# Block table of a state-space layer: stationary and moving operands exchanged, transpose and replication rearranged

## What is computed

```
a_bar = exp(lam * dt)                      # 64 groups x 64 states, complex
b_bar = ((a_bar - 1) / lam) * b
x_t   = a_bar * x_{t-1} + b_bar u_t
y_t   = real(c x_t) + d * u_t
```

## Time and profile before

| | before |
|---|---|
| median of 3 runs | 1712.96 us (1708.61 to 1714.38) |
| the profiled execution | 1714.38 us, span of its trace 1712.3 us |
| PE busy | 1648.0 us, 96% |
| PEld busy | 1381.5 us, 81% |
| DVE busy | 1108.1 us, 65% |
| ACT busy | 945.7 us, 55% |
| POOL busy | 161.4 us, 9% |
| PE on the chain that ended last | 81% of the span |

### The profile page before, as it was taken

How to read it: one execution, slowest core, us unless ns; L and a number is a source line. 1 busy time by engine, 2 the same in 40 slices (tenths; PEclk the granted TensorE clock), 3 DMA queues, 4 the chain that set the end, 5 groups by cost and what they waited for, 6 DMA issues and landing times.

```text
span 1712.3 us, 22507 instructions
## 1 busy us (share of the span) xinstructions
PE 1648.0 (96%) x8994; PEld 1381.5 (81%) x8994; DVE 1108.1 (65%) x1566; ACT 945.7 (55%) x1576; POOL 161.4 (9%) x192
## 2 busy tenths in 40 slices
PE   9999999998999999999989999999999989999997
PEld 7788799786887787878768888788889889788886
DVE  5555667779677554868665556655557686655555
ACT  6455566654567685451465556755555554555545
POOL 0000000208001122710010000100000000000000
PEclk9999999999999999999989999999999999999999
DMA  6755443553455454441445555465554423455552
GB/s 239 265 183 189 169 153 144 179 197 148 174 195 184 176 187 147 180 172 51 160 154 197 178 194 186 158 222 186 194 188 157 148 100 128 176 196 190 187 188 98
DMA packets 50200, 295.93 MB, mean 173 GB/s; under 512 B 5976, under 2 KB 12592, under 8 KB 16432
## 3 DMA queue, kind: packets, MB, share of 16 engines
q1 hardware_dynamic: 49648, 293.86, 47.9%
q0 software_dynamic: 160, 0.52, 0.1%
q10 hardware_dynamic: 288, 0.11, 0.0%
HBM read 293.39 MB, written 1.09 MB: 172 GB/s over the span
## 4 chain that ended last, share of the span: by engine, by line
PE 81%; DVE 9%; ACT 6%; issue 2%; DMA 1%; SPq 1%; POOL 1%; DVEq 0%; POOLq 0%; ACTq 0%
PE PS L2064 77%; DVE wlo L1282 2%; PE PS L2287 2%; DVE wlo L1288 1%; ACT whi L717 1%; PE PS L2209 1%; DMA raw<-in_w 1%; ACT SC L924 1%; ACT whi L721 1%; PE PS L2067 1%; DVE SC L1746 1%; ACT wk L756 0%; PE PS L2460 0%; DVE X L1374 0%; ACT SC L1152 0%
## 5 line engine op out<-in xcount | busy, mean ns | idle before, releaser
L1288 DVE SCALAR_TENSOR_TENSOR wlo<-raw,ct,whi 128x512 fp32r<-128x512 f32 (+1 forms) x552 | 429.5, 827 | 288.0 <-ACT whi L721 287.7
L2064 PE MATMUL PS<-whi,xhi 128*128 128x512 f32 (+2 forms) x1328 | 514.0, 396 | 12.9 <-DVE wlo L1288 4.6
L721 ACT ACTIVATE whi<-raw,ct 128x512 fp32r<-128x512 f32 (+1 forms) x552 | 378.0, 734 | 246.1 <-PE PS L2064 203.5
L2064 PE MATMUL PS<-wlo,xhi 128*128 128x512 f32 (+2 forms) x1328 | 503.9, 389 | 0.0
L1282 DVE TENSOR_TENSOR wlo<-raw,whi 128x1024 fp32r<-128x1024 f32 x240 | 300.0, 1257 | 226.9 <-ACT whi L717 226.2
L2064 PE MATMUL PS<-whi,xlo 128*128 128x512 f32 (+2 forms) x1328 | 413.2, 389 | 0.0
L717 ACT ACTIVATE whi<-raw 128x1024 fp32r<-128x1024 f32 x240 | 252.1, 1057 | 270.7 <-PE PS L2064 201.6
L2064 PEld LDWEIGHTS PS<-whi,xhi 128*128 128x128 f32 x1328 | 251.1, 190 | 68.7 <-issue 8.5
L2064 PEld LDWEIGHTS PS<-whi,xlo 128*128 128x128 f32 x1328 | 251.5, 190 | 52.0
L2064 PEld LDWEIGHTS PS<-wlo,xhi 128*128 128x128 f32 x1328 | 252.2, 190 | 48.0
L2064 PE MATMUL PS<-whi,hhi 128*128 128x512 f32 x544 | 174.4, 395 | 5.2 <-DVE hlo L1453 5.2
(11 more groups left out here) (275 smaller groups left out, 1516.2 us busy)
## 6 DMA issues: line engine op xcount, KB each, us to landing
raw<-in_w SPq DMA_DIRECT2D x263, 1024.0 KB, 4.8
gr<-in_rows SPq DMA_DIRECT2D x14, 512.0 KB, 3.7
SC<-scratch SPq DMA_DIRECT2D x1, 2048.0 KB, 9.9
SC<-scratch SPq DMA_DIRECT2D x2, 1024.0 KB, 9.9
X<-in_x SPq DMA_DIRECT2D x2, 512.0 KB, 5.4
raw<-in_w SPq DMA_DIRECT2D x2, 512.0 KB, 7.1
xn<-in_sc SPq DMA_DIRECT2D x2, 512.0 KB, 3.9
out<-xn SPq DMA_DIRECT2D x4, 256.0 KB, 2.0
```

The source lines that it names most:

```text
L721: e = a.activation(hi[:, f], src[:, f], ACT.Copy, scale=ct[:, c:c + 1])
L1288: e = v.scalar_tensor_tensor(lo[:, f], src[:, f], ct[:, c:c + 1], hi[:, f].bitcast(f32), MUL, SUB)
L2064: return pe.matmul(o, l, r, start=start, stop=stop)
```

## The change

The matmuls of the table exchange their operands: `cst` (128 columns) is now stationary, and `c0` (32 columns) moves. The result for a pair is then 128 partitions (step s, channel) by 32 columns, already in the orientation of `kb`, so the block transpose of VectorE goes. VectorE instead builds `dd` for 16 pairs at a time on 32 partitions and adds it to the tau = 0 part on the way from PSUM into `kb`. ScalarE copies tau = 1 to 3 from PSUM to their places (6 copies of 32x512 for each half), and then the tau = 0 block to the three other places on the diagonal (3 copies). The steps of the tasks move, and the array of d is laid out in another way on the host (the same size as before).

```diff
@@ scalar, tables()
             def tables():
                 for _ in range(6):
                     yield
-                for _ in range(6):
-                    yield
                 for i in range(2):
+                    P = slice(16 * i, 16 * i + 16)
+                    kp = PS[:, 7, :].rearrange("p (i n) -> p i n", i=16)
+                    for _ in range(10):
+                        yield
+                    q.wait_ge(s_kp, i + 1)
+                    q.wait_ge(s_zk, 1)
+                    for tau in range(1, T):
+                        for s in range(T - tau):
+                            r = 32 * (T - 1 - tau)
+                            e = a.activation(kb[32 * s:32 * s + 32, P, s + tau, :], kp[r:r + 32], ACT.Copy)
+                        if tau == T - 1:
+                            e.then_inc(s_k5, 1)
+                        yield
                     q.wait_ge(s_k0, i + 1)
-                    q.wait_ge(s_zk, 1)
-                    for n in range(4):
-                        for s in range(T):
-                            src = ktau[i][32 * n:32 * n + 32, :, s:T, :][:, :, ::-1, :]
-                            e = a.activation(kb[32 * s:32 * s + 32, 16 * i + n:16 * i + 16:4, s:T, :], src, ACT.Copy)
-                            if s % 2:
-                                if n == 3 and s == 3:
-                                    e.then_inc(s_kb, 1)
-                                yield
+                    for s in range(T - 1):
+                        e = a.activation(kb[32 * s:32 * s + 32, P, s, :], kb[96:128, P, T - 1, :], ACT.Copy)
+                    e.then_inc(s_kb, 1)
+                    yield
@@ vector, tables()   (after step 6, which negates c0)
-                q.wait_ge(l_id, 16)
-                after_own()
-                link(v.tensor_reduce(one32, idt.rearrange("p (e c) -> p c e", e=4), AX.X, ADD))
-                tt(dd, one32[:, None, :].to_broadcast([128, 8, 32]), dsk[:, 0:8, None].to_broadcast([128, 8, 32]), MUL)
-                for _ in range(5):
-                    yield
                 for i in range(2):
+                    P = slice(16 * i, 16 * i + 16)
+                    kp = PS[:, 7, :].rearrange("p (i n) -> p i n", i=16)
+                    q.wait_ge(l_id, 16)
+                    if i:
+                        q.wait_ge(s_k0, i)
+                    tt(dd[96:128], idt[96:128, None, 96:128].to_broadcast([32, 16, 32]), dsk[96:128, P, None].to_broadcast([32, 16, 32]), MUL)
+                    for _ in range(9):
+                        yield
                     q.wait_ge(s_kp, i + 1)
-                    v.transpose(ktau[i].rearrange("p q s n -> p (q s n)"), PS[:, 7, :]).then_inc(s_kt, 1)
-                    q.wait_ge(s_kt, i + 1)
-                    tt(ktau[i][:, :, T - 1, :], ktau[i][:, :, T - 1, :], dd[:, 4 * i:4 * i + 4, :], ADD, s_k0)
-                    for _ in range(6):
+                    q.wait_ge(s_zk, 1)
+                    tt(kb[96:128, P, T - 1, :], kp[96:128], dd[96:128], ADD, s_k0)
+                    yield
+                    for _ in range(4):
                         yield
@@ tensor, tables()
             def tables():
-                for _ in range(7):
+                for _ in range(6):
                     yield
                 q.wait_ge(s_sp, 4)
                 q.wait_ge(s_c0, 1)
                 for i in range(2):
                     if i:
-                        q.wait_ge(s_kt, 1)
-                    for n in range(4):
+                        q.wait_ge(s_k0, 1)
+                        q.wait_ge(s_k5, 1)
+                    for n in range(16):
                         for k in range(2):
-                            for m in range(4):
-                                j = 16 * i + 4 * n + m
-                                r = cst[:, k, j, :, :].rearrange("p s n -> p (s n)")
-                                e = mm(PS[32 * m:32 * m + 32, 7, 128 * n:128 * n + 128], c0[k][:, j, :], r, k == 0, k == 1)
-                        if n == 3:
+                            l = cst[:, k, 16 * i + n, :, :].rearrange("p s n -> p (s n)")
+                            e = mm(PS[:, 7, 32 * n:32 * n + 32], l, c0[k][:, 16 * i + n, :], k == 0, k == 1)
+                        if n == 15:
                             e.then_inc(s_kp, 1)
                         if n % 2:
                             yield
-                    for _ in range(4 - i):
-                        yield
-                for _ in range(10):
-                    yield
-                q.wait_ge(s_kt, 2)
-                q.wait_ge(s_kb, 2)
+                    for _ in range(6):
+                        yield
+                q.wait_ge(s_k0, 2)
+                q.wait_ge(s_k5, 2)
                 for i in range(0, 32, 2):
```

More of the change, by code:

```diff
@@ L277, in program @@
             ("sc", "add", "max", "exp", "rc", "at", "pt", "aT", "av", "sq", "r", "on", "xt", "oh", "ol"))
-        s_turn, s_rho, s_e1, s_rot, s_dec, s_sc, s_c0, s_k0, s_kt, s_wT, s_xr, m_gg, m_av2, m_sf = (
-            sem(n) for n in ("s_turn", "s_rho", "s_e1", "s_rot", "s_dec", "s_sc", "s_c0", "s_k0", "s_kt", "s_wT", "s_xr", "m_gg", "m_av2", "m_sf"))
+        s_turn, s_rho, s_e1, s_rot, s_dec, s_sc, s_c0, s_k0, s_k5, s_wT, s_xr, m_gg, m_av2, m_sf = (
+            sem(n) for n in ("s_turn", "s_rho", "s_e1", "s_rot", "s_dec", "s_sc", "s_c0", "s_k0", "s_k5", "s_wT", "s_xr", "m_gg", "m_av2", "m_sf"))
         s_vc, s_gc, s_sin, s_zc, s_zk, s_sp, s_kp, s_kb, s_wt, s_wl, s_cst = (
@@ L374, in program @@
         g_t1 = p16(SC[:, small_at + 64:small_at + 64 + 512])
-        cut = Cut(4096)
-        ktau = [cut(512).rearrange("p (q s n) -> p q s n", q=4, s=T) for _ in range(2)]
-        dd, one32 = p32(cut(256)), cut(32)
+        dd = p32(SC[:, small_at + 64:small_at + 64 + 512])
         uS = xn.rearrange("p h (i n) -> p h i n", i=32)
@@ L1018, in tables @@
                     yield
-                for _ in range(6):
-                    yield
-                for i in range(2):
-                    q.wait_ge(s_k0, i + 1)
-                    q.wait_ge(s_zk, 1)
-                    for n in range(4):
-                        for s in range(T):
-                            src = ktau[i][32 * n:32 * n + 32, :, s:T, :][:, :, ::-1, :]
-                            e = a.activation(kb[32 * s:32 * s + 32, 16 * i + n:16 * i + 16:4, s:T, :], src, ACT.Copy)
-                            if s % 2:
-                                if n == 3 and s == 3:
-                                    e.then_inc(s_kb, 1)
-                                yield
+                for i in range(2):
+                    P = slice(16 * i, 16 * i + 16)
[11 more added lines that the diff above has]
+                        yield
+                    q.wait_ge(s_k0, i + 1)
+                    for s in range(T - 1):
+                        e = a.activation(kb[32 * s:32 * s + 32, P, s, :], kb[96:128, P, T - 1, :], ACT.Copy)
+                    e.then_inc(s_kb, 1)
+                    yield
                 for i in range(0, 32, 2):
@@ L1696, in tables @@
                 yield
-                q.wait_ge(l_id, 16)
-                after_own()
-                link(v.tensor_reduce(one32, idt.rearrange("p (e c) -> p c e", e=4), AX.X, ADD))
-                tt(dd, one32[:, None, :].to_broadcast([128, 8, 32]), dsk[:, 0:8, None].to_broadcast([128, 8, 32]), MUL)
-                for _ in range(5):
-                    yield
-                for i in range(2):
-                    q.wait_ge(s_kp, i + 1)
-                    v.transpose(ktau[i].rearrange("p q s n -> p (q s n)"), PS[:, 7, :]).then_inc(s_kt, 1)
-                    q.wait_ge(s_kt, i + 1)
-                    tt(ktau[i][:, :, T - 1, :], ktau[i][:, :, T - 1, :], dd[:, 4 * i:4 * i + 4, :], ADD, s_k0)
-                    for _ in range(6):
+                for i in range(2):
+                    P = slice(16 * i, 16 * i + 16)
[6 more added lines that the diff above has]
+                        yield
+                    q.wait_ge(s_kp, i + 1)
+                    q.wait_ge(s_zk, 1)
+                    tt(kb[96:128, P, T - 1, :], kp[96:128], dd[96:128], ADD, s_k0)
+                    yield
+                    for _ in range(4):
                         yield
@@ L2923, in layout @@
     dsk = np.zeros((128, 32), np.float32)
-    dsk[:, 0:8] = i["ssm_d"][0].reshape(8, 4, 32).transpose(1, 2, 0).reshape(128, 8)
+    dsk[:, :] = np.tile(i["ssm_d"][0].reshape(32, 32).T, (4, 1))
     par = np.stack([st(i["ssm_lam_re"][0]), st(i["ssm_lam_im"][0]), ldt, dsk])
```

## The result

The changed kernel takes 1723.49 us in the median of 4 runs (1721.64 to 1726.32), the kernel before 1713.07 us (1708.61 to 1714.38). The ratio is 1.0059, with a 95% interval of 1.0038 to 1.0081: slower by some 10 us (6.5 to 14). Forecast were 1723.8 us. Five more executions of the changed kernel are on record, from 1717.20 to 1724.95 us; the median of all nine is 1721.64 us.

A forecast was written before the change was run, and what follows sets the result against it. TensorE, busy in all of 26.00 us from 605 to 631, was taken as the bound. At 0.111 us a row, 14.2 - 3.4 = +10.8 us on the median 1712.96 gave 1723.8 us, range 1719 to 1728.

The forecast's parts named there:

- The price of a row: TensorE's table products: a row costs 0.111 us, set by the load of 128 stationary columns; bounds 0.027 and 0.125.
- the rival in which moving columns set the price: Table products: load hidden, a row costs 0.027 to 0.06 us, total 1713 to 1717 us; chance 0.08.
- All of it on the path: Work inserted into TensorE's program behind about 586 us moves the end one for one, unless it removes a wait.
- The sum for the back part: From the first down unit on: 14 steps of eight rows cost 12.4 us, in place of 3.6 us for three old bursts.
- The front: Before the first down unit: TensorE waits for negated `c0`, then runs 16 rows, and begins that unit 1.95 us late.
- rival at 0.18: TensorE's clock falls after the new gap of about 1.8 us, losing 1.7 us: 1725.5 us; chance 0.18.
- the slack of 5.4 us: ScalarE's spare time in splitting weights, so its bunched copies cost nothing; rival of late ScalarE: 2.5 to 5 us more, 0.06.
- VectorE and GpSimd: VectorE's new work, about 2.7 us for 2.8, and GpSimd's later end, with about 30 us of cover left, cost nothing.

The follow-up runs named there:

- copies twice: The kernel after with each of ScalarE's twelve table copies out of PSUM made twice, the second into free memory; ratio 1.0126 to the kernel before.
- single steps: The kernel before with transposes into wl only in steps no other transposes follow at once, the second step behind a down unit left empty; ratio 0.9992.
- the last one: The kernel before with the second step behind a down unit left empty and each table half in one burst of 64 rows; ratio 0.9979.

## Why the prediction was right

The mechanism held: products that lie on TensorE's path in full, at the price of a load of 128 columns, and a wait for `c0` in front. That the median of four executions lies only 0.3 us from the forecast is luck, for the interval of the difference is 6.5 to 14 us, and the parts of the sum were off by some 0.4 us in the back part and up to 0.7 us in the front.

**The price of a row** was the main term, and it held: 0.111 us predicted from products with 64 moving columns, 0.111 measured with 32. The reason given was the load of 128 columns. Doubling the moving side changed the back part by 0.02 us, halving the stationary side brought the row to 0.059; that refutes the rival in which moving columns set the price. That it is the load, and nothing else that grows with the stationary columns, rests on the loads' own records: 192 ns for 128 columns and 137 for 64, so 0.055 us for 64 columns. The 60 cycles that the Trainium skill names as the floor of a matmul (TensorEngine Tiling (Array Packing), Instruction Overhead), an estimate of 25 ns, don't set the price of this shape either, as 0.111 us shows. The same page of the Trainium skill, in When to Use Tiling, advises to exchange the operands where 32 columns move; that is borne out in bursts of 32 rows, by 0.038 us a row against 0.111.

**All of it on the path.** The sum for the back part was 12.4 - 3.6 = 8.8 us; it grew by 9.17. The sum left out that each burst also delays the second weight matmul behind it by 0.09 us. Leaving nearly all of the products out gave back 11.9 us, with 0.1 us more of waits in their place.

**The front** was forecast at +1.95 us. The wait for `c0` is there, but this pair of executions shows it at 1.27 us, not the 1.8 to 2.1 forecast, and the front only 0.45 longer. The two can't be compared as they are. The granted clock at the stage's start was at its lower level in the kernel before already during the eight transposes (1.97 us), in the kernel after only behind them (1.32 us). The busy times of the first microsecond, with the granted clock third from the end, before:

```profile
559.00:560.00 1.00, 0.73 (x4) 0.73 (x5) 1.00 (x3) 0.72 (x2) 0.18 (x1) 0.50 0.88 365
```

and after:

```profile
553.00:554.00 1.00, 0.92 (x6) 0.68 (x7) 1.00 (x3) 0.77 (x3) 0.36 (x1) 1.00 0.96 307
```

Where the transposes lasted 1.97 us, the front was 26.98 us before and 28.97 in the run with copies twice, whose front has the same instructions as that of the kernel after, with a wait of 1.80 us for `c0`. Where they lasted 1.32 to 1.35, it was 25.85 with single steps (the front of the kernel before) and 27.43 and 27.14 in the kernel after and with 64 moving columns. So like against like the front costs 1.3 to 2.0 us: the forecast of 1.95 was right for the clock that my rows showed and 0.4 to 0.7 us too large for the other. With 9.2 us of the back part this makes 10.5 to 11.2 us, inside the measured interval. With so few executions at each clock this is a working from five profiles, not a test of its own.

**The clock** didn't fall in the new gap (rival at 0.18): it was 1.00 from 575 to 580 us and after.

```profile
575.00:580.00 5.00, 4.05 (x24) 3.56 (x24) 4.94 (x8) 2.29 (x5) 0.00 (x0) 1.00 0.37 115
```

**ScalarE** wasn't late, as forecast, but much nearer to it than I wrote. For `wlo` no wait came even with the copies made twice, so nothing speaks against the slack of 5.4 us there. But I overlooked that the products at step 21 and the first transposes hang on ScalarE's own order, with 1.3 us of slack and with none. In the second half it works without a pause through its copies and splits. The first four transposes run from 649.28 to 649.88, and ScalarE is free to copy them out at 649.91:

```profile
648.57 1.34 ACT L719 ACTIVATE whi<-raw,ct 128x512 fp32r<-128x512 f32 x2
649.91 0.60 ACT L1038 ACTIVATE SC<-PS 128x512 f32<-128x512 f32 x1
651.26 0.60 ACT L1038 ACTIVATE SC<-PS 128x512 f32<-128x512 f32 x1 [0.75 <-PE PS L2463]
```

The 0.69 us that TensorE then waits is little more than the copy itself (0.60), as at the three other places and as before the change. A little more work on ScalarE there would have shown at once.

**VectorE and GpSimd** cost the back part 0.2 us at the most, where the forecast was nothing: with the old products and all else new it was 178.74 us, of which one burst of 1.2 us came out of the front.

## What to carry to other kernels

Where TensorE is full, price a small product by both sides, stationary and moving columns, and take the larger, which held for the shapes of this case. Taking a transpose off an engine with idle time isn't worth longer loads on the engine that bounds. Narrow stationary tiles are cheap when a long burst fills all column groups, and dear in many short ones. To see an effect of half a per cent in a profile, cut the stage out between two fixed instructions and compare executions that entered it at the same clock.

## What the runs showed of the hardware beyond this

- A burst of 128-column products fits between weight matmuls with no fixed cost: 0.90 us for eight rows at 0.111. Narrow tiles have one: with 64 stationary columns 0.77 us for eight rows at 0.059, so 0.3 us beyond the rows; with 32 columns and 32 rows 1.20 us, of which the rows' distances of 0.026 us make 0.8, so 0.4 us.
- Tiles of 32 stationary columns on different column groups run side by side, and a burst is as long as the rows of one group. With 128 moving columns the bursts last 0.64 us (eight rows, four in each of two groups), 0.66 (16 rows, four in each of four groups), 1.08 (32 rows, eight in each) and 1.95 (64 rows, 16 in each). So one more row in every group adds 0.105 to 0.109 us, about the 0.108 us of a transpose with 128 moving columns.
- The transposes' loads of 128 columns last 140 ns, those of products 190, and 64 moving columns cost no more than 32 with the latter (back part 186.52 us against 186.50).
- Once TensorE became faster in this layer, a new wait of 0.8 us for `hlo` came in both kernels that removed time here, and in the chain of the last one it hangs on a weight DMA: the stream of weights is the next bound.
